# PEER mixer with 384 dense prompt columns instead of 416, gates from bf16 one-hots in three parts, and another layout of the scratch in HBM

## The chip, the cores and the metric

The kernel runs on one core of a Trainium2 chip, in one launch. The metric is the device time of that launch in microseconds (us), as the median of three runs. Engines are named as in the profile: PE (TensorE), DVE (VectorE), ACT (ScalarE), POOL (GpSimd), SP (SyncE, which here only issues DMAs).

## The reference

One inference step of a two-layer decoder: 512 prompt tokens and 8 sample tokens. Layer 0 mixes tokens with a chunked gMLP, layer 1 with sparse attention; behind each stands the PEER channel mixer, which is what the change is about. It finds 16 experts of 16384 for each of 8 heads of a token and adds up their outputs. The block is computed as:

```
PEER_HEADS = 8
N_KEYS = 128
PEER_TOPK = 16

        v1, i1 = lax.top_k(s1, PEER_TOPK)
        v2, i2 = lax.top_k(s2, PEER_TOPK)
        cand = (v1[..., :, None] + v2[..., None, :]).reshape(PEER_BLOCK, PEER_HEADS, PEER_TOPK * PEER_TOPK)
        cand_idx = (i1[..., :, None] * N_KEYS + i2[..., None, :]).reshape(PEER_BLOCK, PEER_HEADS, PEER_TOPK * PEER_TOPK)
        top_s, top_pos = lax.top_k(cand, PEER_TOPK)
        eidx = jnp.take_along_axis(cand_idx, top_pos, axis=-1)
        gate = jax.nn.softmax(top_s, axis=-1)
        u = expert_u[eidx]
        act = jax.nn.gelu(jnp.einsum('thkd,td->thk', u, xb))
        vv = expert_v[eidx]
        return jnp.einsum('thk,thkd->td', (gate * act).astype(vv.dtype), vv)
```

All numbers are float32. `expert_u` and `expert_v` have 16384 rows of 1024 numbers for each layer, 67 MB each.

## The kernel before

**Two ways to one sum.** For the last ND = 416 prompt tokens (the dense columns, `D0` to `TP`) the kernel computes the activations of all 16384 experts and multiplies them by a gate that is zero for those not chosen. For the first D0 = 96 prompt tokens and the 8 sample tokens (the sparse ones) it fetches the chosen rows alone. Activations are held transposed: experts on the partitions, tokens in the columns.

**Slabs.** The weights come in slabs of 128 x 1024 floats (512 KB). SP loads them into a ring of four `raw` buffers (L473; the next load of a buffer waits until the slab before it in that buffer is used). ACT rounds each to `w_hi` (L1104), POOL or, in the output stage, DVE makes the rest, `w_lo` (L2274, L1955), two slabs ahead of PE. A slab in `dense` (L638) is 24 matmuls: 8 pieces x (hi x hi, hi weights x low input, low weights x hi input), each with ND columns.

**The score stage of a layer (s0, s1: 128 slabs of `u`).** PE multiplies slab n (`s_slab`), ACT takes the gelu (L1236) and SP stores it to `act_d` (L513). Between the slabs the gates are made, by four blocks of 128 prompt tokens. A block has
- score matmuls of all keys (L814, 16 matmuls), which ACT copies to `sc` (L1288);
- a routing window of `ROUTE_SLABS` slabs (20, 16, 16, 16). In it DVE finds the 16 experts a head: `chosen` with its MAX8, FIND_INDEX8 and MATCH_REPLACE8 (L1711 to L1724), the sums of candidates `cand` (L1739), the sixteen rounds of L1773 and L1777, and `shares` (L1785 to L1789), which ends with `route_done`;
- three transposes of `route` (L825) on PE, which wait for `route_done`, and copies of them by ACT to `idxT` and `gateT` (L1309, L1313), which end with `slotT_done`;
- gate steps (`STEPS_OF`: 4 in block 0, since only its last 32 tokens are dense, then 16, 16, 16). In a step of 8 tokens PE does one slab and then 8 gate matmuls (`gates`, L774): for each token, a one-hot of the first key index by a one-hot of the second that carries the gate. Both one-hots are made by DVE (`one_hots`: L1873 for `hot`, L1876 eight times for `hot_gate`), in two buffers. They compare with `count_row`, a copy of `iota` in PSUM (the tile `misc`, L1799). ACT copies the result to `gout` (L1249), and SP stores each second step to `gate_d` (L524).

After the last gate step, the slabs left are plain (8 of them).

**The sparse tokens.** They are worked in groups of 16 entries of the list (`NGR` = 7 groups: one of the samples, six of 16 prompt tokens each), 16 picks a group, so NDOT = 112 dots and 112 values a layer. For each, POOL issues an indirect DMA that gathers 128 rows (64 for the samples) of 4 KB into one of four `rows` buffers (L2308). A dot is one DVE operation over 1024 elements (L1838), against the group's inputs, which lie in PSUM. They are laid out on SBUF by `group_rows` (`hS`, L1824) and turned by PE (`group_h`, L796). Which dot stands where is written in tables: 12 in each window (`WINDOW_DOTS`; DVE does one at each call of `between`, and there are 12 calls in a routing), `STEP_DOTS` in the gate steps. `FETCH_AT` puts each fetch on POOL two slabs before. The indices of the prompt's sparse tokens go by HBM: after block 0's `route_done` SP stores `route` to `route_d` (L530), waits for it, and reads it back in another order with 24 transfers (L534) into `routeP`, of which DVE makes `expertP` (L1913).

**The output stage (y0, y1: 128 slabs of `v`).** In groups of 8 slabs, ACT's queue loads the activations and gates back (`abuf`, `gbuf`), DVE multiplies them (`weigh`, L1940), ACT and POOL split the product (L1278, L2316), PE multiplies (L638), DVE adds to `x` (L1984). DVE also makes `w_lo` there and adds one gathered row a slab to the sum of the sparse group (`value`, L1857). A finished group goes by ACT to `v_out`, by PE (`group_y`, L843) to PSUM, by DVE to `x`. Eight weighings and eight low parts (L1947) stand before the first slab.

## Time and profile before

| | |
|---|---|
| time, median of 3 runs (lowest to highest) | 3715.84 us (3708.44 to 3722.89) |
| the profiled execution, its span | 3715.8 us |
| PE busy | 3517.8 us, 95% |
| DVE busy | 2481.2 us, 67% |
| ACT busy | 1361.9 us, 37% |
| POOL busy | 1842.5 us, 50% |
| s0, y0 | 439.9 to 1173.1 us, 1175.3 to 1774.2 us |
| s1, y1 | 2366.7 to 3095.2 us, 3097.4 to 3699.1 us |
| moved by DMA | 812.36 MB, mean 219 GB/s |

The stages are cut at the first and the last slab matmul (L638) of each. Busy time adds the instructions of an engine; a PE record of a pipelined matmul is longer than the step from one matmul to the next, so the rate is read from the starts. "Idle before" in brackets is the time an engine waited and what ended it.

### The profile page before, as it was taken

How to read it: one execution, taken by the hardware profiler on the slowest of the kernel's cores; microseconds unless marked ns; L12 is line 12 of the kernel's file. 1: busy time of each engine (PE TensorE's matmuls, PEld its weight loads, DVE VectorE, ACT ScalarE, POOL GpSimd, SP SyncE). 2: the span in 40 equal slices, each digit the busy share in tenths (PEclk: the TensorE clock that was granted, in tenths of full speed). 3: DMA queues.
4: the chain of work that ended last, by engine and by line, in shares of the span. 5: the costliest groups of instructions: out<-in, count | busy, mean ns of one | idle time of the engine just before them, and what ended most of it. 6: DMA issues, size and time to landing. Idle time of an engine off the chain costs nothing.

```text
span 3715.8 us, 61775 instructions
## 1 busy us (share of the span) xinstructions
PE 3517.8 (95%) x21277; PEld 3348.0 (90%) x21277; DVE 2481.2 (67%) x5400; ACT 1361.9 (37%) x1938; POOL 1842.5 (50%) x1172
## 2 busy tenths in 40 slices
PE   7999999999999999999888689999999999999998
PEld 7999999999999999999773359999999999999998
DVE  3342597777775777775678543679697876777774
ACT  3322343534444333333221353344435353333332
POOL 3434456555655555552541234456565655555551
PEclk9999999999999999999998699999999999999999
DMA  3222367877788999994346322467777879999982
GB/s 131 80 69 91 103 188 247 277 247 262 262 281 274 298 310 313 324 320 154 99 116 179 105 74 91 136 193 249 268 240 277 274 282 277 297 326 311 329 295 97
DMA packets 392484, 812.36 MB, mean 219 GB/s; under 512 B 52104, under 2 KB 249672, under 8 KB 384888
## 3 DMA queue, kind: packets, MB, share of 16 engines
q1 hardware_dynamic: 171600, 458.35, 37.0%
q0 software_dynamic: 64608, 230.73, 18.1%
q10 hardware_dynamic: 156048, 120.37, 11.0%
q8 instruction: 127, 2.08, 0.2%
q14 instruction: 101, 0.83, 0.1%
HBM read 695.39 MB, written 112.74 MB: 217 GB/s over the span
## 4 chain that ended last, share of the span: by engine, by line
PE 66%; DVE 16%; DMA 7%; issue 4%; ACT 2%; POOL 2%; SPq 2%; another core or an unknown queue 0%; ACTq 0%; DVEq 0%; POOLq 0%
PE acc L638 42%; PE acc L625 15%; DMA rows<-u_in,expertP 4%; PE misc L774 3%; DVE rows L1838 3%; DMA raw<-slabs_in 2%; POOL w_lo L2274 1%; DVE misc L1773 1%; DVE route L1777 1%; DVE hot_gate L1876 1%; PE misc L814 1%; ACT w_hi L1104 1%; DVE work L1716 1%; DVE keyi L1724 1%; PE misc L843 1%
## 5 line engine op out<-in xcount | busy, mean ns | idle before, releaser
L2274 POOL TENSOR_TENSOR w_lo<-raw,w_hi 128x1024 fp32r<-128x1024 f32 x365 | 892.6, 2446 | 1079.8 <-ACT w_hi L1104 1078.6
L638 PE MATMUL acc<-h_hi,w_hi 128*128 128x416 f32 x3072 | 1097.7, 357 | 0.2 <-POOL h_lo L2316 0.2
L638 PE MATMUL acc<-h_lo,w_hi 128*128 128x416 f32 x3072 | 1085.9, 353 | 0.0
L638 PE MATMUL acc<-h_hi,w_lo 128*128 128x416 f32 x3072 | 1081.2, 352 | 0.0
L1104 ACT ACTIVATE w_hi<-raw 128x1024 fp32r<-128x1024 f32 x617 | 653.3, 1060 | 1090.0 <-DMA raw<-slabs_in 1045.4
L638 PEld LDWEIGHTS acc<-h_hi,w_hi 128*128 128x128 f32 x3072 | 581.2, 189 | 8.5 <-POOL h_lo L2316 0.6
L638 PEld LDWEIGHTS acc<-h_hi,w_lo 128*128 128x128 f32 x3072 | 581.9, 189 | 7.4
L638 PEld LDWEIGHTS acc<-h_lo,w_hi 128*128 128x128 f32 x3072 | 581.3, 189 | 3.9
L1955 DVE TENSOR_TENSOR w_lo<-raw,w_hi 128x1024 fp32r<-128x1024 f32 x252 | 325.4, 1291 | 206.1 <-ACT w_hi L1104 205.5
L1838 DVE CUSTOM_DVE_ANT_0 rows<-acc,rows 128x1024 f32<-128x1024 f32 (+1 forms) x224 | 273.4, 1221 | 205.9 <-DMA rows<-u_in,expertP 183.7
L638 PE MATMUL acc<-y_hi,w_hi 128*128 128x416 f32 x1024 | 362.1, 354 | 10.3 <-DVE y_lo L1947 4.3
L1236 ACT ACTIVATE gelu<-acc 128x416 f32<-128x416 f32 x256 | 132.5, 517 | 649.1 <-PE acc L638 588.4
L638 PE MATMUL acc<-y_hi,w_lo 128*128 128x416 f32 x1024 | 361.3, 353 | 0.0
L638 PE MATMUL acc<-y_lo,w_hi 128*128 128x416 f32 x1024 | 358.4, 350 | 0.0
L2316 POOL TENSOR_TENSOR h_lo<-abuf,h_hi 128x416 fp32r<-128x416 f32 x128 | 208.6, 1630 | 234.2 <-ACT h_hi L1278 232.3
L2316 POOL TENSOR_TENSOR y_lo<-abuf,y_hi 128x416 fp32r<-128x416 f32 x112 | 180.2, 1609 | 234.0 <-ACT y_hi L1278 233.1
L1876 DVE TENSOR_SCALAR hot_gate<-misc,idxT,gateT 128x128 f32<-128x128 f32 x832 | 273.8, 400 | 0.0
L1984 DVE TENSOR_TENSOR x<-x,acc 128x416 f32<-128x416 f32 x256 | 148.9, 582 | 128.0 <-PE acc L638 122.3
L625 PE MATMUL acc<-h_hi,w_hi 128*128 128x260 f32 x912 | 191.7, 292 | 40.0 <-DVE rb L2019 16.7
L1249 ACT ACTIVATE gout<-misc 128x512 f32<-128x512 f32 x208 | 205.4, 1065 | 58.2 <-PE misc L774 50.9
L774 PEld LDWEIGHTS misc<-hot_gate,hot 128*128 128x128 f32 x1664 | 199.5, 191 | 30.1 <-issue 26.6
L774 PE MATMUL misc<-hot_gate,hot 128*128 128x128 f32 x1664 | 205.1, 276 | 20.9 <-DVE hot_gate L1876 14.0
(349 smaller groups left out, 5549.4 us busy)
## 6 DMA issues: line engine op xcount, KB each, us to landing
raw<-slabs_in SPq DMA_DIRECT2D x617, 512.0 KB
act_d<-gelu SPq DMA_DIRECT2D x256, 208.0 KB
gate_d<-gout SPq DMA_DIRECT2D x52, 1024.0 KB
abuf<-act_d ACTq DMA_DIRECT2D x32, 1664.0 KB
gbuf<-gate_d ACTq DMA_DIRECT2D x30, 1664.0 KB
unit<-ck_in SPq DMA_DIRECT2D x72, 128.0 KB
vquad<-cv_in SPq DMA_DIRECT2D x64, 128.0 KB
unit<-ck_in ACTq DMA_DIRECT2D x56, 128.0 KB
```

The costliest lines, as they stand in the source:

```text
L625: last = pe.matmul(acc[:, par, half, 0:HT], w[:, c, :], m(c)[:, half * HT:(half + 1) * HT], start=start and c == 0 and w is w_hi[r] and m ...
L638: last = pe.matmul(acc[:, 0, par, 0:ND], w[:, c, :], m(c), start=c == 0 and w is w_hi[r] and m is m_hi, stop=c == KC - 1 and w is w_lo[r])
L774: last = pe.matmul(misc[:, q, j * P:(j + 1) * P], hot1[par][:, t, :], hot_gate[par][:, t, :], start=True, stop=True)
L1104: act.activation(w_hi[r][:], raw[r][:], ACT.Copy).then_inc(hi_done, 1)
L1236: act.activation(gelu[:, par, :], acc[:, 0, par, 0:ND], ACT.Gelu_apprx_tanh).then_inc(acc_free_act, 1)
L1249: act.activation(gout[cpar][:, :, t0:t0 + 4].rearrange("p i t -> p t i"), misc[:, q, :].rearrange("p (t i) -> p t i", t=4), ACT.Copy).then ...
L1838: dve.tensor_tensor_reduce(out=row, in0=acc[0:n, 1], in1=row, scale=1.0, scalar=0.0, op0=ALU.mult, op1=ALU.add, accum_out=dots[0:n, g, k:k ...
L1876: last = dve.tensor_scalar(hot_gate[par][:, t, :], count_row, idxT[:, 1, t0 + t:t0 + t + 1], gateT[:, t0 + t:t0 + t + 1], ALU.is_equal, AL ...
L1955: dve.tensor_tensor(w_lo[r][:], raw[r][:], w_hi[r][:].bitcast(F32), ALU.subtract).then_inc(lo_done, 1)
L1984: dve.tensor_tensor(x[:, c, D0:TP], x[:, c, D0:TP], acc[:, 0, c % 2, 0:ND], ALU.add).then_inc(acc_free_dve, 1)
L2274: pool.tensor_tensor(w_lo[r][:], raw[r][:], w_hi[r][:].bitcast(F32), ALU.subtract).then_inc(lo_done, 1)
L2316: pool.tensor_tensor(y_lo[par][:, c, 0:ND], abuf[par][:, c, :], y_hi[par][:, c, 0:ND].bitcast(F32), ALU.subtract).then_inc(y_lo_done, 1)
```

## The change

- **Columns.** `ND` goes from 416 to 384, so `D0` from 96 to 128: block 0 is sparse as a whole. The sparse groups become 9 (`NGR`), dots and values 144 a layer each. Block 0 loses its transposes, copies and 4 gate steps; PE waits for its `route_done` ahead of block 1's score matmuls, since the same PSUM banks hold what DVE works on. Gate steps are 16 in each of blocks 1 to 3, and 12 plain slabs follow.
- **Tables.** 16 dots in block 0's window and 12 in the others, then 24 in each block's gate steps, and 20 behind the last. Values: 11 for each 9 slabs (`values_by`). The groups' ends follow from it (`GROUP_END`).
- **Order at the end of s.** DVE weighs the first group of eight before it makes `weights`, and ACT's gelu of the dots stands behind the last slab.
- **One-hots.** `idxT`, `gateT` and the one-hots become bf16, laid out with the 8 tokens of a step innermost; `iota8` is a bf16 count in SBUF in that form, made by one DVE copy at the start of `peer`. The gate is split into three bf16 parts (`gate_parts`, once a block). A step is five DVE operations of 128 x 1024 (two comparisons, three products), and on PE 24 matmuls of 128 columns, three for each token. `count_row` is gone.
- **Scratch.** `act_d` holds four slabs side by side for a partition and `gate_d` is ordered by the group that reads it, so that loads run over 6 KB and 12 KB in a row, while a store of gates has runs of 512 bytes.

```diff
@@ -49,7 +49,7 @@
-ND = 416
+ND = 384
@@ -218,33 +218,34 @@
-        topd = take("topd", [P, PH, TOPK])
...
+        topd = route[:, 2]
...
-        idxT = take("idxT", [P, 2, ND])
-        gateT = take("gateT", [P, ND])
+        idxT = take("idxT", [P, 2, ND], BF16)
+        gateT = take("gateT", [P, 3, ND], BF16)
+        iota8 = take("iota8", [P, P, TG // 2], BF16)
...
-        hot1 = [take(f"hot1_{r}", [P, HG, P]) for r in range(2)]
-        hot_gate = [take(f"hot_gate{r}", [P, HG, P]) for r in range(2)]
+        hot1 = [take(f"hot1_{r}", [P, P, HG], BF16) for r in range(2)]
+        hot_gate = [take(f"hot_gate{r}", [P, 3, P, HG], BF16) for r in range(2)]
@@ -365,8 +366,8 @@
-        act_d = [nc.dram_tensor(f"act_d{l}", [NK, P, ND], F32).ap() for l in range(2)]
-        gate_d = [nc.dram_tensor(f"gate_d{l}", [NG, P, NK, TG], F32).ap() for l in range(2)]
+        act_d = [nc.dram_tensor(f"act_d{l}", [NK // 4, P, 4, ND], F32).ap() for l in range(2)]
+        gate_d = [nc.dram_tensor(f"gate_d{l}", [NK // GRP, P, NG, GRP, TG], F32).ap() for l in range(2)]
@@ -452,17 +453,27 @@
-        WINDOW_DOTS = 12
-        STEP_DOTS = [[1] * 4, [1] * 4 + [0, 0] + [2, 1, 2, 1, 2, 2, 1, 2, 1, 2]]
...
+        WINDOW_DOTS = [16, 12, 12, 12]
+        STEP_DOTS = [[], [1] * 4 + [2] * 8 + [1] * 4, [1] * 8 + [2] * 8, [1, 2] * 8]
...
+        TAIL_DOTS = NDOT - len(at_slab)
+        at_slab += [S_DONE + i * (NK - S_DONE - 3) // TAIL_DOTS for i in range(TAIL_DOTS)]
...
+        def values_by(n):
...
+            return min(NDOT, ((n + 1) * 11 + 8) // 9)
...
+        at_slab += [NK + n for n in range(NK) for _ in range(values_by(n) - (values_by(n - 1) if n else 0))]
...
+        GROUP_END = [next(n for n in range(NK) if values_by(n) >= (g + 1) * TOPK) for g in range(NGR)]
@@ -521,7 +532,8 @@
-                    sp.dma_start(gate_d[l][chunk], gout[cpar][:]).then_inc(gate_stored[cpar], 16)
+                    sp.dma_start(gate_d[l][:, :, chunk].rearrange("j p g t -> p j (g t)"),
+                                 gout[cpar][:].rearrange("p (j g) t -> p j (g t)", g=GRP)).then_inc(gate_stored[cpar], 16)
@@ -771,8 +784,9 @@
-                            last = pe.matmul(misc[:, q, j * P:(j + 1) * P], hot1[par][:, t, :],
-                                             hot_gate[par][:, t, :], start=True, stop=True)
+                            for part in range(3):
+                                last = pe.matmul(misc[:, q, j * P:(j + 1) * P], hot1[par][:, :, t],
+                                                 hot_gate[par][:, part, :, t], start=part == 0, stop=part == 2)
@@ -796,18 +810,21 @@
+                    if b == 1:
+                        pe.wait_ge(route_done, B)
@@ -816,21 +833,43 @@
-                    s_only(2)
-                    group_h(2 * b - 1 if b else 0)
-                    s_only(ROUTE_SLABS[b] - 2)
+                        s_only(2)
+                        group_h(0)
+                        s_only(ROUTE_SLABS[0] - 2)
+                        continue
+                    if b == 1:
+                        s_only(2)
+                        group_h(1)
+                        s_only(ROUTE_SLABS[b] - 2)
+                    if b == 2:
+                        s_only(ROUTE_SLABS[b])
+                    if b == 3:
+                        s_only(12)
+                        group_h(6)
+                        s_only(ROUTE_SLABS[b] - 12)
...
-                    if b:
+                    if b == 1:
...
-                        group_h(2 * b)
-                        steps(b, 4, STEPS_OF[b] - 4)
-                    else:
-                        steps(b, 0, STEPS_OF[b])
+                        group_h(2)
+                        steps(b, 4, 12)
+                        group_h(3)
+                        steps(b, 12, 16)
+                    if b == 2:
+                        group_h(4)
+                        steps(b, 0, 12)
+                        group_h(5)
+                        steps(b, 12, 16)
+                    if b == 3:
+                        steps(b, 0, 8)
+                        group_h(7)
+                        steps(b, 8, 16)
+                s_only(2)
+                group_h(8)
@@ -1255,12 +1295,12 @@
-                    act.dma_start(abuf[par][:], act_d[l][j * GRP:(j + 1) * GRP].rearrange("i p t -> p i t")).then_inc(
+                    act.dma_start(abuf[par][:].rearrange("p (b i) t -> p b (i t)", b=2),
+                                  act_d[l][2 * j:2 * j + 2].rearrange("b p i t -> p b (i t)")).then_inc(
...
-                    act.dma_start(gbuf[par][:], gate_d[l][:, :, j * GRP:(j + 1) * GRP, :].rearrange(
-                        "n p i t -> p n i t")).then_inc(group_loaded[par], 16)
+                    act.dma_start(gbuf[par][:], gate_d[l][j]).then_inc(group_loaded[par], 16)
@@ -1295,22 +1334,25 @@
+                    if b == 0:
+                        continue
...
-                    act.activation(gateT[:, lo - D0:t0 + P - D0], misc[:, 2, 2 * P + lo - t0:3 * P], ACT.Copy).then_inc(
+                    act.activation(gateT[:, 0, lo - D0:t0 + P - D0], misc[:, 2, 2 * P + lo - t0:3 * P], ACT.Copy).then_inc(
@@ -1324,10 +1366,6 @@
-                act.wait_ge(rows_used, l * OPS + NDOT)
-                act.activation(dots[0:SR, 0], dots[0:SR, 0], ACT.Gelu_apprx_tanh).then_inc(dot_act_done, 1)
-                act.activation(dots[:, 1:NGR], dots[:, 1:NGR], ACT.Gelu_apprx_tanh).then_inc(dot_act_done, 1)
@@ -1349,6 +1387,10 @@
+                act.wait_ge(rows_used, l * OPS + NDOT)
+                act.activation(dots[0:SR, 0], dots[0:SR, 0], ACT.Gelu_apprx_tanh).then_inc(dot_act_done, 1)
+                act.activation(dots[:, 1:NGR], dots[:, 1:NGR], ACT.Gelu_apprx_tanh).then_inc(dot_act_done, 1)
@@ -1865,17 +1906,38 @@
+            def gate_parts(b):
...
+                t0 = max(b * P, D0)
+                c0, c1 = t0 - D0, (b + 1) * P - D0
+                gate = misc[:, 2, 2 * P + t0 - b * P:3 * P]
+                left = rest[:, t0 - b * P:P]
+                dve.tensor_tensor(left, gate, gateT[:, 0, c0:c1], ALU.subtract).then_inc(dve_step, step.up())
+                dve.wait_ge(dve_step, step.at)
+                dve.tensor_copy(gateT[:, 1, c0:c1], left).then_inc(dve_step, step.up())
+                dve.wait_ge(dve_step, step.at)
+                dve.tensor_tensor(gateT[:, 2, c0:c1], left, gateT[:, 1, c0:c1], ALU.subtract).then_inc(parts_done, 1)
+                dve.wait_ge(parts_done, n_parts[0] + 1)
+                n_parts[0] += 1
...
-                dve.tensor_tensor(hot1[par][:], count_row.unsqueeze(1).to_broadcast([P, HG, P]),
-                                  idxT[:, 0, t0:t0 + HG].unsqueeze(2).to_broadcast([P, HG, P]), ALU.is_equal)
-                for t in range(HG):
-                    last = dve.tensor_scalar(hot_gate[par][:, t, :], count_row, idxT[:, 1, t0 + t:t0 + t + 1],
-                                             gateT[:, t0 + t:t0 + t + 1], ALU.is_equal, ALU.mult)
-                last.then_inc(hot_done, 1)
+                of = [P, P, HG]
+                dve.tensor_tensor(hot_gate[par][:, 2], iota8[:], idxT[:, 1, t0:t0 + HG].unsqueeze(1).to_broadcast(of),
+                                  ALU.is_equal).then_inc(dve_step, step.up())
+                dve.tensor_tensor(hot1[par][:], iota8[:], idxT[:, 0, t0:t0 + HG].unsqueeze(1).to_broadcast(of),
+                                  ALU.is_equal)
+                dve.wait_ge(dve_step, step.at)
+                for part in range(2):
+                    dve.tensor_tensor(hot_gate[par][:, part], hot_gate[par][:, 2],
+                                      gateT[:, part, t0:t0 + HG].unsqueeze(1).to_broadcast(of),
+                                      ALU.mult).then_inc(dve_step, step.up())
+                dve.wait_ge(dve_step, step.at)
+                dve.tensor_tensor(hot_gate[par][:, 2], hot_gate[par][:, 2],
+                                  gateT[:, 2, t0:t0 + HG].unsqueeze(1).to_broadcast(of), ALU.mult).then_inc(hot_done, 1)
@@ -1918,13 +1983,17 @@
-                    dve.wait_ge(slotT_done, B + 1)
+                        continue
+                    dve.wait_ge(slotT_done, l * (NDB - 1) + b)
+                    gate_parts(b)
...
-                        for _ in range(STEP_DOTS[b > 0][r]):
+                        for _ in range(STEP_DOTS[b][r]):
...
+                while done[0] < NDOT:
+                    next_dot()
@@ -1955,15 +2024,15 @@
+                for c in range(GRP):
+                    weigh(0, c)
+                for c in range(GRP):
+                    low_part(0, c)
...
-                for c in range(GRP):
-                    weigh(0, c)
-                for c in range(GRP):
-                    low_part(0, c)
@@ -1974,10 +2043,10 @@
-                    if n < NDOT:
-                        value(l, n)
-                    if n % TOPK == 10 and 0 < n // TOPK <= NGR:
-                        group_add(l, n // TOPK - 1)
+                    for i in range(values_by(n - 1) if n else 0, values_by(n)):
+                        value(l, i)
+                    if n - 5 in GROUP_END:
+                        group_add(l, GROUP_END.index(n - 5))
```

On DVE, in a gate step of block 1 (`rows`, `dots`: a dot; `hot`, `hot_gate`: the one-hots; `iota_119` is `iota8`), before:

```order
L1838 ISA rows_133,dots<-acc,rows_133 64x1024
L1838 ISA dots 64x1
L1873 TENSOR_TENSOR hot_1_125<-misc,idxT 128x1024
L1876 TENSOR_SCALAR hot_gate_127<-misc,idxT,gateT 128x128 x8
L1913 SCALAR_TENSOR_TENSOR expertP<-routeP 128x96
```

and after:

```order
L1879 ISA rows_130,dots<-acc,rows_130 128x1024
L1879 ISA dots 128x1
L1929 TENSOR_TENSOR hot_gate_125<-iota_119,idxT 128x1024
L1931 TENSOR_TENSOR hot_0_123<-iota_119,idxT 128x1024
L1935 TENSOR_TENSOR hot_gate_125<-hot_gate_125,gateT 128x1024 x2
L1939 TENSOR_TENSOR hot_gate_125<-hot_gate_125,gateT 128x1024
```

One operation of 1024 elements that reads PSUM and eight of 128 have become five of 1024 elements with both inputs in SBUF. (The rows of before are the last step of block 0, which has the same form, with `expertP` behind it.)

On DVE, from the end of block 0's routing to the start of block 1's. Before, its last share (`route<-route,gsum`) is followed by the samples' shares and the first gate step; three more steps stand ahead of `expertP` and of the next MAX8:

```order
L1789 TENSOR_TENSOR route<-route,gsum 128x128
L1785 TENSOR_REDUCE gsumS<-routeS 64x1
L1787 RECIPROCAL gsumS<-gsumS 64x1
L1789 TENSOR_TENSOR routeS<-routeS,gsumS 64x16
L1838 ISA rows_130,dots<-acc,rows_130 64x1024
L1838 ISA dots 64x1
L1873 TENSOR_TENSOR hot_0_124<-misc,idxT 128x1024
L1876 TENSOR_SCALAR hot_gate_126<-misc,idxT,gateT 128x128 x8
```

After:

```order
L1831 TENSOR_TENSOR route<-route,gsum 128x128
L1879 ISA rows_129,dots<-acc,rows_129 64x1024
L1879 ISA dots 64x1
...
L1879 ISA rows_132,dots<-acc,rows_132 64x1024
L1879 ISA dots 64x1
L1827 TENSOR_REDUCE gsumS<-routeS 64x1
L1829 RECIPROCAL gsumS<-gsumS 64x1
L1831 TENSOR_TENSOR routeS<-routeS,gsumS 64x16
L1978 SCALAR_TENSOR_TENSOR expertP<-routeP 128x128
L1753 MAX keyv<-sc 128x8 x16
```

Four dots have moved behind the last share, and `expertP` follows them with no gate step between.

On DVE, at the end of the score stage. Before:

```order
L1873 TENSOR_TENSOR hot_1_125<-misc,idxT 128x1024
L1876 TENSOR_SCALAR hot_gate_127<-misc,idxT,gateT 128x128 x8
L1959 TENSOR_TENSOR weights<-dots,routeS 64x16
L1961 TENSOR_TENSOR weights<-dots,routeP 128x96
L1940 TENSOR_TENSOR abuf_146<-abuf_146,gbuf_147 128x416 x8
```

After, where twenty dots stand between the last one-hots and these rows:

```order
L1879 ISA rows_132,dots<-acc,rows_132 128x1024
L1879 ISA dots 128x1
L2009 TENSOR_TENSOR abuf_145<-abuf_145,gbuf_146 128x384 x8
L2016 TENSOR_TENSOR y_lo_148<-abuf_145,y_hi_147 128x384 x8
L2032 TENSOR_TENSOR weights<-dots,routeS 64x16
L2034 TENSOR_TENSOR weights<-dots,routeP 128x128
```

The weighing of the first eight slabs now stands behind all dots and ahead of `weights`.

## Rows read from the trace of the kernel before

**Rows 1.** The page: busy us and share of the span, by engine.

```profile
PE 3517.8 (95%) x21277; PEld 3348.0 (90%) x21277; DVE 2481.2 (67%) x5400; ACT 1361.9 (37%) x1938; POOL 1842.5 (50%) x1172
```

**Rows 2.** Stages by windows: length, busy PE, PEld, DVE, ACT, POOL, clock, DMA share, GB/s.

```profile
439.90:1173.10 733.20, 705.14 (x4071) 692.24 (x4069) 563.47 (x1730) 329.53 (x414) 417.52 (x241) 0.99 0.75 250
1175.30:1774.20 598.90, 596.89 (x3184) 588.68 (x3184) 431.67 (x496) 198.70 (x262) 314.77 (x232) 1.00 0.86 283
2366.70:3095.20 728.50, 702.55 (x4071) 689.78 (x4069) 563.36 (x1730) 328.97 (x415) 418.75 (x241) 0.99 0.75 251
```

**Rows 3.** Windows of s0: routing and gate steps of block 1, routing of block 2.

```profile
568.00:644.00 76.00, 73.40 (x392) 72.21 (x390) 63.42 (x265) 28.58 (x37) 53.35 (x30) 1.00 0.76 239
644.00:758.00 114.00, 109.10 (x685) 106.81 (x686) 84.30 (x185) 56.29 (x70) 55.36 (x34) 0.99 0.77 269
758.00:837.00 79.00, 73.61 (x392) 72.42 (x392) 65.89 (x265) 28.66 (x37) 52.90 (x30) 0.99 0.76 243
```

**Rows 4.** Timeline, end of block 2's window on PE; waits of DVE, 644 to 758.

```profile
836.76 0.90 PE L825 MATMUL misc<-ident,route 128*128 128x128 f32 x3 [5.39 <-DVE route L1789]
...
DVE rows L1838 <- DMA rows<-u_in,expertP: 20.8, 11, 5.8
```

**Rows 5.** Timeline of PE (start, length): matmuls of 260 and of 416 columns.

```profile
319.73 0.40 PE L625 MATMUL acc<-g_hi,w_hi 128*128 128x260 f32 x2
319.97 0.40 PE L625 MATMUL acc<-g_lo,w_hi 128*128 128x260 f32 x2
...
1499.95 0.35 PE L638 MATMUL acc<-y_hi,w_lo 128*128 128x416 f32 x1
1500.14 0.35 PE L638 MATMUL acc<-y_hi,w_hi 128*128 128x416 f32 x1
```

**Rows 6.** Timeline, hand-over from block 0 to block 1, on DVE, SP and POOL.

```profile
529.61 1.89 DVE L1789 TENSOR_TENSOR route<-route,gsum 128x128 f32<-128x128 f32 x1
...
533.24 0.33 SPq L530 DMA_DIRECT2D route_d<-route  x1
538.56 12.94 SPq L534 DMA_DIRECT2D routeP<-route_d  x24
...
553.25 0.24 DVE L1913 SCALAR_TENSOR_TENSOR expertP<-routeP 128x96 uint32<-128x96 f32 x1
568.50 0.29 DVE L1799 COPY misc<-iota 128x128 f32<-128x128 f32 x1 [15.01 <-ACT sc L1288]
...
576.57 0.97 POOL L2308 DMA_INDIRECT rows<-u_in,expertP  x1
...
582.34 1.22 DVE L1838 CUSTOM_DVE_ANT_0 rows<-acc,rows 128x1024 f32<-128x1024 f32 x1 [10.46 <-DMA rows<-u_in,expertP]
```

**Rows 7.** Timeline of one gate step of block 2, on PE, DVE, ACT and POOL.

```profile
884.29 2.05 PE L774 MATMUL misc<-hot_gate,hot 128*128 128x128 f32 x16 [1.01 <-DVE hot_gate L1876]
886.09 0.43 PE L638 MATMUL acc<-h_hi,w_hi 128*128 128x416 f32 x1
...
886.36 1.21 DVE L1873 TENSOR_TENSOR hot<-misc,idxT 128x1024 f32<-128x1024 f32 x1
887.49 2.63 DVE L1876 TENSOR_SCALAR hot_gate<-misc,idxT,gateT 128x128 f32<-128x128 f32 x8
890.04 1.21 DVE L1838 CUSTOM_DVE_ANT_0 rows<-acc,rows 128x1024 f32<-128x1024 f32 x1
...
893.54 1.08 ACT L1104 ACTIVATE w_hi<-raw 128x1024 fp32r<-128x1024 f32 x1
...
894.70 2.41 POOL L2274 TENSOR_TENSOR w_lo<-raw,w_hi 128x1024 fp32r<-128x1024 f32 x1 [2.81 <-ACT w_hi L1104]
```

**Rows 8.** Timeline: a cast, `cand` without and behind POOL's `w_lo`, a tensor_tensor.

```profile
512.24 0.42 DVE L1777 TENSOR_TENSOR route<-misc,route 128x256 f32<-128x256 f32 x1
...
604.63 1.15 DVE L1739 TENSOR_TENSOR cand<-keyv 128x512 f32<-128x512 f32 x2
...
796.34 0.29 DVE L1733 CAST keyf<-keyi 128x256 f32<-128x256 uint32 x1
796.55 3.36 DVE L1739 TENSOR_TENSOR cand<-keyv 128x512 f32<-128x512 f32 x2
...
796.88 2.61 POOL L2274 TENSOR_TENSOR w_lo<-raw,w_hi 128x1024 fp32r<-128x1024 f32 x1 [1.27 <-ACT w_hi L1104]
```

**Rows 9.** The page: queues (packets, MB, share); then y0's first window.

```profile
q1 hardware_dynamic: 171600, 458.35, 37.0%
q0 software_dynamic: 64608, 230.73, 18.1%
q10 hardware_dynamic: 156048, 120.37, 11.0%
...
1173.00:1300.00 127.00, 123.11 (x644) 120.31 (x644) 91.98 (x107) 41.20 (x56) 74.36 (x55) 0.99 0.96 290
```

58 lines of the change are left out of this document (32 added, 26 removed).

## The prediction

> **What bounds the kernel now.** I read the engine line of the page first: PE is busy for 95% of the span [rows 1]. A busy PE alone does not say what a narrower matmul is worth, so I cut the span by stage [rows 2]: in each layer the score stage (s, 128 slabs through `s_slab`) takes 733 or 729 us and the output stage (y, 128 slabs) 599 or 602, together 2662 of 3715.8 us. In y PE is all but continuously busy. In s it is not, and the stretches tell why [rows 3]. A block of 128 prompt tokens has two parts: a routing window of 16 slabs, in which DVE picks experts, and 16 gate steps, each a slab and eight gate matmuls. Block 2's window ends with PE waiting 5.4 us for DVE's last routing row [rows 4]. So windows are DVE's, gate steps and y are PE's.
>
> **Columns: 416 to 384.** Matmuls of 416 columns start 0.19 us apart, those of 260 columns 0.12 [rows 5]. The line through both gives 0.45 ns a column, so 32 columns are 14 ns, and a slab of 24 matmuls takes 4.22 us in place of 24 x 0.19 = 4.56. For 512 slabs that is 174 us if PE set the pace everywhere. What is left of it is the question.
>
> **Windows of blocks 2 and 3** (78 us each, [rows 3]) are not shortened: PE's 16 slabs get 5.5 us faster and it waits 5.5 us longer. DVE's own work is the same 12 dots and the same picks. Its first dot waits 10.5 us (block 1's in [rows 6]) for rows that Pool asks for one slab into the window; that slab is 0.3 us shorter. I take -0.5 us a window, -1 a layer.
>
> **The hand-over from block 0.** Before, four gate steps and block 1's scores stand between DVE's `route_done` (531.5) and its next routing (568.5) [rows 6]. Now block 0 has no gate steps. What is late next is `routeP`: SP stores the routes at 533.24, waits until 538.56 and issues 24 transfers for 12.94 us, to 551.50; with some 2 us of landing (an estimate, from the `expertP` row at 553.25, which may have found them already there) DVE can go on at 553.5, 22 us after `route_done`. Four more dots (4 x 1.22) lie behind `route_done` and inside this wait, so they cost nothing. The copy into `iota8` costs about 1.2 us ahead of it (as the 1024-element rows of [rows 7]). SP issues no slab loads meanwhile, but PE has 15 us of slack here. Block 1's first dot then waits about 2 us and not 10.5, as Pool can fetch right behind `expertP` (0.97 to issue at 576.57, 4.8 to land by 582.34, less 3.2 of MAX8). Sum: DVE starts 15 - 1.2 = 14 us earlier and needs 8 us less: **-22 us**.
>
> **Gate steps.** From 644 to 758 us are block 1's 16 steps and block 2's scores, 114 us [rows 3]. Three changes:
> - PE: the slab, -0.34. The gate matmuls were 16 records in 1.8 us, from 884.29 to the next slab's matmul at 886.09 [rows 7]; now 24 matmuls of 128 columns in one pass. The line of rows 5 gives 62 ns for 128 columns, 1.5 us; the fp32 record's 0.112 us gives 2.7. All operands are now read with a step of 16 bytes, which no row shows. I stay between, at 1.8, and count no change: it leans to the line, as the operands are no longer fp32.
> - DVE: one `hot` of 1.13 and eight `hot_gate`, 3.68 us from 886.36 to 890.04, become five tensor_tensor of 1024 bf16 elements. At the fp32 rate they are 1.14 apart, at two elements a cycle 0.60. That the engine has such a rate is seen in the cast of 256 elements in 0.29 us, while a tensor_tensor of 256 takes 0.42 [rows 8]. I take 0.60: 3.2 us with two waits. Dots rise from 1.25 to 1.5 a step, 1.8 us. Total 5.1 us against PE's 4.22 + 1.8 = 6.0, so nothing on the path.
> - Three small operations of `gate_parts` (about 0.9 us with their waits) stand before the first one-hots of a block. Before, the first one-hots were there 1.4 (waiting) + 1.2 (a dot) + 3.7 = 6.3 us after the route, now 1.4 + 0.9 + 1.2 + 3.2 = 6.7; and PE, which already waited for them, is there 0.34 earlier. So PE waits 0.8 more a block. One more `group_h` is 0.9.
>
> A block's steps: -5.5 + 0.8 + 0.9 = **-3.8 us**, three blocks **-11**.
>
> The Trainium skill ("VectorE: DVE Perf Modes", The perf-mode tier table) gives a bf16 tensor_tensor from SBUF twice the fp32 rate; no operation of the kernel before shows it, and by the page the sum would stay as above.
>
> **The tail of s.** Slabs left after the last gate step are 12, not 8: 12 x 4.22 - 8 x 4.56 = +14.2, and one `group_h`, 0.9. This is where the four steps saved in block 0 come back as plain slabs. Twenty dots lie there now, two for each slab. Behind them stand the eight weightings that the y stage needs; I add 4 us of late start. Tail: **+19**. Two dots a step also load the DMA queues more; +5 for rows that come late (in block 1's steps DVE already waits 20.8 us for rows [rows 4], but it has slack).
>
> s stage: -22 - 1 - 11 + 19 + 5 = **-10 us** a layer. Most of the narrower matmul is given back, to DVE in the windows.
>
> **The y stage.** PE: -128 x 0.34 = -44; two more `group_y` with 1.8 us of PE each, +3.5. DMA: of [rows 9], q10 moves 120.4 MB for 11.0% of 16 engines, 18.4 GB/s an engine; q1 20.8, q0 21.4. One y stage before: 67 MB of slabs, 55 MB of activations and gates (at q10's rate) and 55 MB of expert rows, 8730 engine-us, 546 us of the 599. After: 50 MB in long runs at q1's rate, 71 MB of expert rows: 8980, 561 us, while PE's time falls to 599 - 44 + 3.5 = 559. The measured share (0.86 of 599 is 515) is 0.94 of what this reckoning gives, so 529 of 559. It is full, not over. I add 5 us for slabs that come late. DVE, a slab: 0.50 + 1.14 + 0.47 + 1.22 values x 1.21 = 3.6 (starts 0.07 us before the one ahead ends, lengths as n/0.96 + 0.07 us fits the rows of [rows 7]), under 4.22. y: -44 + 3.5 + 5 = **-35 us** a layer.
>
> **Sum**: 2 x (-10 - 35) = -90, so 3715.8 - 90 = 3626 us. The profiled execution (3715.8) is the median of the runs (3715.84). Under 0.5% (19 us) a measurement of this kernel can't tell a change from none.
>
> **Rivals.**
> 1. *Gate matmuls at 0.112 us.* Reading every eighth bf16 may hold PE at the fp32 pace or below. 24 x 0.112 = 2.7, +0.9 on 96 steps = +86: **3712**, no change. Against it: an fp32 element takes two passes, bf16 one. The Trainium skill ("Advanced Engine Details and Errata", Memory Cachelines) says that SBUF lines have 16 bytes and an access that hits a new line each time pays; here each element of both operands is on a line of its own. No row shows its price. Chance 0.17.
> 2. *Transfers set y's pace.* The share is 0.96 in y's first 127 us now [rows 9]. If it can't rise, y stays near 599 us: 3626 + 70 = **3696**, at the edge of no change. Chance 0.11.
> 3. *The port between DVE and Pool (slower).* `cand` reads two SBUF operands, and the second of its two operations came behind Pool's `w_lo`: 3.36 us for two, where they take 1.2 when Pool is idle [rows 8]. So one waits for the other to end. The one-hots before read `misc` (PSUM); all five now read SBUF twice, and Pool's 2.4 us `w_lo` comes in each step, at 894.70, 1.1 us after `w_hi` [rows 7]. Alone this fits: 3.2 + 2.4 = 5.6 of 6.0, with the dots (PSUM and SBUF) under `w_lo`. It decides when dots come late by more than the 2.6 us by which DVE is ahead: then `w_lo` falls into the burst in each step and a step is 3.2 + 2.4 + 1.9 = 7.5, +1.5 on 96 steps = +144: **3770**. Chance 0.10.
> 4. *The fast rate isn't taken* (the change does not do what it says, also slower). Five at 1.14 and Pool's 2.4 shut out of them: 8.3 a step, +2.3 x 96 = +221: **3847**. For it: one operand of each is a row of eight read again and again, of which the trace has none. Chance 0.06.
>
> **How the numbers follow.** Forecast 3626, its own range 3585 to 3672 (gate matmuls at 62 ns give 3599, late rows and a late start of y up to +45), chance 0.56. Range for 8 in 10: from 3585 to 3765, which takes in rivals 1 and 2 and the milder half of 3. Faster by over 0.5% (below 3697): the forecast, and part of rivals 1 and 2, 0.65. Within: 0.18. Slower: rivals 3 and 4 and the top of 1, 0.17.
>
> **What would show it.** Matmuls of 384 columns 175 ns apart. PE waiting at `route_done` for 6 to 8 us in block 0, 12 to 16 in block 1, some 10 in blocks 2 and 3. The DVE tensor_tensor of the one-hots at 0.6 to 0.7 us; many over 2 us would be rival 3, all at 1.2 rival 4. The gap between a gate step's slabs, 1.8 us now: over 2.5 is rival 1. In y, slab starts 4.22 us apart; if the DMA share is at 0.97 and PE idles before slabs, rival 2. Wrong would be above all the assumption that DVE's windows don't move, and that the dots' rows keep up.

## The result: 4273.6 us, 15% slower

The changed kernel takes 4273.58 us (median of 4 runs, 4269.2 to 4275.98) against 3716.28: a ratio of 1.150, 95% interval 1.148 to 1.153. The forecast was 3626, its range ended at 3765. The profiled execution has a span of 4270.4 us, and its stages are cut as before.

The engine line of the page, of after (it answers to [rows 1]):

```profile
PE 3921.3 (92%) x22007; PEld 3557.3 (83%) x22007; DVE 2701.8 (63%) x5156; ACT 1354.8 (32%) x1922; POOL 1929.7 (45%) x1300
```

PE is busy for 404 us more, though its slab matmuls are narrower. The windows view by stage, of after (columns as in [rows 2]; y0, y1, s0, s1):

```profile
1424.00:2054.00 630.00, 579.53 (x3216) 568.45 (x3216) 488.23 (x532) 198.34 (x264) 308.76 (x263) 0.97 0.81 289
3628.60:4257.60 629.00, 579.98 (x3216) 571.78 (x3216) 477.71 (x529) 192.14 (x255) 311.20 (x261) 0.97 0.81 287
440.80:1420.70 979.90, 925.57 (x4404) 815.04 (x4402) 620.04 (x1571) 326.07 (x402) 461.94 (x274) 0.86 0.62 200
2643.10:3625.40 982.30, 924.22 (x4403) 813.21 (x4402) 624.01 (x1570) 325.93 (x402) 463.06 (x274) 0.85 0.62 199
```

Each s stage is 247 to 254 us longer (733 and 729 before), each y stage 31 and 27 longer (599 and 602). These add up to 559 us, and the spans differ by 555: nothing outside the stages grew. In s the granted clock is down from 0.99 to 0.86, in y the DMA share from 0.86 to 0.81. Inside s0, routing of block 1, gate steps of block 1 with block 2's scores, and routing of block 2, the windows that answer to [rows 3]:

```profile
557.00:627.00 70.00, 55.78 (x303) 54.84 (x301) 62.97 (x265) 24.53 (x32) 48.07 (x28) 0.93 0.82 270
627.00:824.00 197.00, 191.00 (x826) 155.72 (x827) 99.84 (x135) 59.24 (x71) 63.38 (x38) 0.78 0.51 160
824.00:896.00 72.00, 66.61 (x380) 66.29 (x380) 60.06 (x263) 27.73 (x36) 51.76 (x30) 0.98 0.81 263
```

The two routing windows are 6 and 7 us shorter. The gate steps take 197 us where they took 114. One of them on PE, by the timeline (it answers to [rows 7]):

```profile
716.83 0.34 PE L651 MATMUL acc<-h_lo,w_hi 128*128 128x384 f32 x1
717.00 0.34 PE L651 MATMUL acc<-h_hi,w_lo 128*128 128x384 f32 x1
717.18 5.81 PE L788 MATMUL misc<-hot_gate,hot 128*128 128x128 bf16 x24
722.63 0.68 PE L651 MATMUL acc<-h_hi,w_hi 128*128 128x384 f32 x1
723.11 0.52 PE L651 MATMUL acc<-h_lo,w_hi 128*128 128x384 f32 x1
723.43 0.52 PE L651 MATMUL acc<-h_hi,w_lo 128*128 128x384 f32 x1
```

From the first gate matmul (717.18) to the next slab (722.63) it is 5.45 us, 0.227 us a matmul; before, the eight took 1.8 in [rows 7] and 1.70 in the median. Then the clock counts as well: slab matmuls start 0.32 us apart behind the gate matmuls (723.11, 723.43), and 0.17 to 0.18 apart at the slab's end (716.83, 717.00), when the upper level is granted again. In 84 of the 96 steps it is 5.43 to 5.46 us: in 4 of them the granted clock stayed at its upper level (2.4 GHz), in 80 it was at the lower (1.2 GHz) for a part. In the other 12 something else of PE's stands before the next slab. Behind the gate matmuls the lower level held for 3.3 us in the median step. The median step is 11.29 us long against 6.31.

### The profile page after: what moved, and what is told of

Same layout as the page of the kernel before. It is cut to its first block, busy times and chain, and to the rows that moved or that the text cites. A ratio compares the mean times of both kernels' runs of the same rounds, so it can differ in the third digit from the quotient of the medians.

```text
span 4270.4 us, 63212 instructions
## 1 busy us (share of the span) xinstructions
PE 3921.3 (92%) x22007; PEld 3557.3 (83%) x22007; DVE 2701.8 (63%) x5156; ACT 1354.8 (32%) x1922; POOL 1929.7 (45%) x1300
## 4 chain that ended last, share of the span: by engine, by line
PE 56%; DVE 22%; DMA 11%; issue 5%; ACT 2%; POOL 2%; SPq 1%; another core or an unknown queue 0%; DVEq 0%; ACTq 0%; POOLq 0%
PE acc L651 24%; PE acc L638 13%; PE misc L788 13%; DMA raw<-slabs_in 8%; DVE rows L1879 3%; DVE w_lo L2024 2%; DMA rows<-u_in,expertP 2%; DVE route L1819 1%; DVE misc L1815 1%; DVE abuf L2009 1%; ACT w_hi L1144 1%; DVE work L1758 1%; DVE keyi L1766 1%; DVE keyi L1757 1%; DVE keyv L1762 1%
## 5 line engine op out<-in xcount | busy, mean ns | idle before, releaser
L651 PE MATMUL acc<-h_hi,w_hi 128*128 128x384 f32 x3072 | 1143.1, 372 | 95.1 <-POOL w_lo L2344 41.8
L651 PE MATMUL acc<-h_lo,w_hi 128*128 128x384 f32 x3072 | 1108.1, 361 | 0.0
L651 PE MATMUL acc<-h_hi,w_lo 128*128 128x384 f32 x3072 | 1105.9, 360 | 0.0
L788 PE MATMUL misc<-hot_gate,hot 128*128 128x128 bf16 x2304 | 557.3, 414 | 18.3 <-DVE hot_gate L1939 18.3
L788 PEld LDWEIGHTS misc<-hot_gate,hot 128*128 128x128 bf16 x2304 | 327.5, 146 | 218.5 <-issue 35.7
L651 PE MATMUL acc<-y_hi,w_hi 128*128 128x384 f32 x1024 | 357.9, 350 | 57.9 <-DVE x L2053 43.3
L2378 POOL DMA_INDIRECT rows<-v_in,expertP x256 | 260.3, 1017 | 232.4 <-DVE misc L1898 103.5
L651 PE MATMUL acc<-y_lo,w_hi 128*128 128x384 f32 x1024 | 354.0, 346 | 0.0
L651 PE MATMUL acc<-y_hi,w_lo 128*128 128x384 f32 x1024 | 353.6, 345 | 0.0
L2378 POOL DMA_INDIRECT rows<-u_in,expertP x256 | 267.9, 1047 | 84.8 <-issue 28.3
```

Source lines behind the costliest of these rows:

```text
L651: last = pe.matmul(acc[:, 0, par, 0:ND], w[:, c, :], m(c), start=c == 0 and w is w_hi[r] and m is m_hi, stop=c == KC - 1 and w is w_lo[r])
L788: last = pe.matmul(misc[:, q, j * P:(j + 1) * P], hot1[par][:, :, t], hot_gate[par][:, part, :, t], start=part == 0, stop=part == 2)
L2378: pool.indirect_dma_start(out=rows[n % RB][0:rows_of], out_offset=None, in_=a[f"v{l}" if half else f"u{l}"], in_offset=bass.IndirectOffset ...
```

## Experiments

All are variants of the changed kernel. "A step" is a gate step, "gates" the time from its first gate matmul to the next slab, in the median. Lengths of stages are those of the profiled execution. Where the text gives no ratio, the time is that of one execution.

| kernel | time, us | gates, us | s0, s1 | y0, y1 |
|---|---|---|---|---|
| before | 3716 | 1.70 | 733, 729 | 599, 602 |
| changed | 4274 | 5.45 | 980, 982 | 630, 629 |
| both operands in a row | 3869 | 1.32 | 780, 775 | 631, 627 |
| moving operand in a row | 3872 | 1.51 | 772, 779 | 636, 631 |
| weights in a row | 4244 | 5.25 | 961, 969 | 634, 626 |
| moving operand, step of 8 bytes | 3918 | 2.87 | 800, 802 | 631, 632 |
| moving operand, step of 4 bytes | 3872 | 1.55 | 784, 775 | 633, 627 |
| roles exchanged | 3912 | 1.51 | 796, 803 | 631, 632 |
| exchanged, other DVE order | 3801 | 1.51 | 749, 747 | 622, 630 |
| scratch of before | 4165 | 5.45 | 970, 979 | 584, 579 |
| long loads in pieces | 4181 | 5.45 | 978, 982 | 587, 584 |
| exchanged, order, scratch of before | 3702 | 1.51 | 736, 741 | 589, 587 |
| exchanged, order, pieces | 3719 | 1.51 | 748, 748 | 585, 584 |
| exchanged, order, hybrid scratch | 3701 | 1.51 | 745, 741 | 586, 584 |
| columns alone | 3702 | 1.80 | 734, 741 | 597, 586 |
| exchanged, order, scratch of before, half the rows | 3703 | 1.51 | 731, 736 | 618, 611 |
| the same, all rows, half the values | 3639 | 1.51 | 739, 732 | 573, 581 |
| exchanged, order, pieces, half the values | 3687 | 1.51 | 742, 741 | 574, 574 |

### What makes the gate matmuls slow

PE reads 128 elements in a row, which belong to other tokens, so these kernels compute other gates; nothing else is changed. The first does it for both operands, the next two for one each:

```diff
-  hot1[par][:, :, t],  hot_gate[par][:, part, :, t]
+  hot1[par][:].rearrange("p k t -> p (k t)")[:, t * P:(t + 1) * P],
+  hot_gate[par][:, part].rearrange("p k t -> p (k t)")[:, t * P:(t + 1) * P]
```

> The changed kernel, but PE reads both operands of the gate matmuls as 128 elements in a row instead of every eighth. The elements are then those of other tokens, so the gates are wrong; DVE, the number of matmuls and all else stay. Theory 1 (the step of 16 bytes between elements is what costs): the 24 gate matmuls of a step fall from 5.45 us to 1.5 to 1.8 us, the clock stays at its upper level in the gate steps, a step falls from 11.3 to about 6 us, and the time from 4274 to about 3755 us (96 x 5.3 less). Theory 2 (24 bf16 matmuls with 24 weight loads cost this in any layout): 5.45 us stays and the time stays at 4274.

> As the run before, but only the moving operand (hot_gate) is read in a row; the weights (hot) keep the step of 16 bytes. Part of the gates is wrong. If the moving operand pays, the 24 matmuls fall to 1.5 to 1.8 us and the time to about 3755; if the weights pay, both stay (5.45 us, 4274). If each alone is slow and the load of weights runs beside the matmul before it, neither run with one operand in a row gains.

> The other half: only the weights (hot) are read in a row, the moving operand keeps the step of 16 bytes. Part of the gates is wrong. If the moving operand pays alone, 5.45 us and 4274 stay; if the weights pay alone, 1.5 to 1.8 us and about 3755.

The moving operand in a row alone takes the gates from 5.45 to 1.51 us and the time from 4274 to 3872; the weights alone take them to 5.25 and the time to 4244. So 24 matmuls and 24 loads of weights are not slow as such, and strided weights cost 0.2 us a step. It is the moving operand, of which a column was fetched every 16 bytes. With it in a row the clock is 0.95 over the run (0.91 in the changed kernel); it fell behind the gate matmuls of 14 steps of 96, and of 92 in the changed kernel: the fall of the clock went with the slow matmuls. The time stopped at 3870, though, 115 us above the 3755 that I had expected. The y stages are as they were, and the expectation had left them so; the 115 us are gate steps of 7.5 us where I had expected 6, which comes below. That other elements are read here is not what makes it fast: the kernels with exchanged roles below compute the right gates and take the same 1.51 us.

```diff
-  hot_gate[par][:, part, :, t]
+  hot_gate[par][:, part].rearrange("p k t -> p (k t)")[:, t * 64:t * 64 + 509:4]   # or 255:2
```

> The changed kernel, but PE reads the moving operand of the gate matmuls with a step of 8 bytes (every fourth bf16) in place of 16; the weights keep 16. The elements are then other ones, so the gates are wrong; all else stays. Theory 1 (each 16-byte piece of SBUF that is opened for one element costs; two elements in one are enough): the 24 matmuls take about 1.5 us and the time is 3872, as with the moving operand in a row. Theory 2 (any step between elements costs, in proportion to the bytes passed over): about 2.7 us, the time about 4000. Theory 3 (any step costs the whole): 5.45 us and 4274.

> The same with a step of 4 bytes (every second bf16). Theory 1: 1.5 us and 3872, as with 8 bytes. Theory 2: 1.5 us (1.36 by proportion, under the rate in a row), 3872. Theory 3: 5.45 us and 4274.

With steps of 16, 8, 4 and 2 bytes the gates take 5.45, 2.87, 1.55 and 1.51 us, so 1.77, 0.93, 0.50 and 0.49 ns a column. The cost goes with the bytes that are passed over, and from 4 bytes down the matmul's own pace rules. Two elements in each 16 bytes are not enough: theory 1 gave 1.5 us for the step of 8 bytes, theory 2 gave 2.7. The time of that kernel, 3918, is 82 us under theory 2's 4000: I had left out the clock, which fell behind the gate matmuls of only 19 of 96 steps here. The Trainium skill ("Advanced Engine Details and Errata", Memory Cachelines) says that one needs two hits on a line of 16 bytes; the trace agrees that one element in 16 bytes is bad (1.77 ns a column against 0.49) and disagrees on two (0.93).

### DVE and POOL shut each other out

With both operands in a row, steps with one dot took from 5.6 us up, those with two dots mostly 7.6. The timeline of such a step in that kernel, DVE, then POOL, then PE:

```profile
695.91 1.22 DVE L1879 CUSTOM_DVE_ANT_0 rows<-acc,rows 128x1024 f32<-128x1024 f32 x1
697.06 0.69 DVE L1929 TENSOR_TENSOR hot_gate<-iota,idxT 128x1024 bf16<-128x1024 bf16 x1
697.66 0.68 DVE L1931 TENSOR_TENSOR hot<-iota,idxT 128x1024 bf16<-128x1024 bf16 x1
698.26 3.47 DVE L1935 TENSOR_TENSOR hot_gate<-hot_gate,gateT 128x1024 bf16<-128x1024 bf16 x2
701.77 0.69 DVE L1939 TENSOR_TENSOR hot_gate<-hot_gate,gateT 128x1024 bf16<-128x1024 bf16 x1
...
698.79 2.40 POOL L2344 TENSOR_TENSOR w_lo<-raw,w_hi 128x1024 fp32r<-128x1024 f32 x1 [2.60 <-ACT w_hi L1144]
...
702.60 0.62 PE L788 MATMUL misc<-hot_gate,hot 128*128 128x128 bf16 x8 [1.84 <-DVE hot_gate L1939]
```

Two products take 3.47 us here and 1.28 to 1.33 elsewhere, with POOL's `w_lo` of 2.40 inside them, and PE waits 1.84 us for the last. It is no single case: in s0 of this kernel, 19 of the 96 first and second products ran beside `w_lo` for over 0.5 us and took 2.88 us in the median, the 57 that never met it 0.68. The dots, which read PSUM and SBUF, took 1.22 beside it (57 of them) and without it (76). The place repeats in each step, since the four engines wait for each other in a ring: `w_lo` for ACT's `w_hi`, ACT for the gate matmuls, PE for DVE, DVE for `w_lo`. That is rival 3 of the prediction, at 7.6 us a step where it said 7.5, but not under its condition, which was that dots come late. Two kernels test it. The first swaps the roles of the one-hots, so that the one in rows moves; the second also changes DVE's order and lets the one in rows read its count from PSUM:

```diff
 # roles exchanged
-  pe.matmul(misc[...], hot1[par][:, :, t], hot_gate[par][:, part, :, t], ...)
+  pe.matmul(misc[...], hot_gate[par][:, part, :, t], hot1[par][:, t, :], ...)
-  dve.tensor_tensor(hot1[par][:], iota8[:], idxT[:, 0, t0:t0 + HG].unsqueeze(1)...)
+  dve.tensor_tensor(hot1[par][:], iota[:].unsqueeze(1)..., idxT[:, 1, t0:t0 + HG].unsqueeze(2)...)
 # other order: comparison and three products, the dots, and last
+  dve.tensor_tensor(hot1[par][:], count_in_psum.unsqueeze(1)..., idxT[:, 1, t0:t0 + HG].unsqueeze(2)...)
```

> The changed kernel with the two one-hots of a token in exchanged roles: the one that carries the three gate parts is loaded as weights, still with a step of 16 bytes, and the other is made in rows (fp32 count in SBUF, bf16 out) and moves. Same numbers, same order, scratch as changed. Theory (only the moving operand's step costs): 24 matmuls in 1.5 us instead of 5.45. With one two-input operation at 1.14 us more in place of one at 0.6, the port theory (DVE's two-SBUF-input operations and POOL's w_lo shut each other out) gives steps with two dots at 3.6 + 2.4 + 1.9 = 7.9 us or more and those with one dot at 6.5 to 7, the time 3890 to 3930. If the port plays no part, DVE needs 5.3 us and PE 5.8 a step, the time is about 3800.

> As the run with exchanged roles, and DVE in another order: the four operations with two SBUF inputs first, then the step's dots, then the one-hot in rows, whose count is read from PSUM, as in the kernel before. So 3.5 us of DVE's work a step have a PSUM input and can lie beside POOL's w_lo of 2.4 us. The port theory gives steps of 5.8 to 6.0 us with one dot or two, and a time of about 3790 us; if the excess over 5.8 us in the steps had another cause (rows that come late, ACT's copies), they stay at 7.6 with two dots and the time at 3870 or more.

The first took 3912 us with a median step of 8.12, the second 3801 with 6.42; both are as the port theory had them, within 11 us. DVE of the second, with two dots in the step (POOL's `w_lo` below it):

```profile
881.17 0.69 DVE L1939 TENSOR_TENSOR hot_gate<-hot_gate,gateT 128x1024 bf16<-128x1024 bf16 x1
881.78 1.22 DVE L1879 CUSTOM_DVE_ANT_0 rows<-acc,rows 128x1024 f32<-128x1024 f32 x1
...
882.92 1.22 DVE L1879 CUSTOM_DVE_ANT_0 rows<-acc,rows 128x1024 f32<-128x1024 f32 x1
...
884.07 1.22 DVE L1943 TENSOR_TENSOR hot<-misc,idxT 128x1024 bf16<-128x1024 f32 x1
885.21 1.39 DVE L1931 TENSOR_TENSOR hot_gate<-iota,idxT 128x1024 bf16<-128x1024 bf16 x1
...
883.65 2.40 POOL L2347 TENSOR_TENSOR w_lo<-raw,w_hi 128x1024 fp32r<-128x1024 f32 x1 [2.31 <-ACT w_hi L1144]
```

POOL's 2.4 us now lie beside a dot and the `hot` that reads PSUM, and nearly nothing is lost: only the comparison at 885.21, which begins before `w_lo` ends (886.05), takes 1.39 in place of 0.68. So 111 us went, with the same number of operations on DVE in a step. Order and source of the operand were changed together, and no run parts them. Steps stay at 6.4 where I had said 6.0, as DVE is busy without a break in those with two dots (6.70 in the median, 5.81 with one).

### The long runs in the scratch

> The changed kernel with act_d and gate_d laid out and loaded as in the kernel before (runs of 1.5 KB and 512 bytes), all else as changed. Theory A (a group's 3 MB in long packets push the slabs' 4 KB packets back, so that slabs come late in bursts): each y stage falls from 630 to about 575 us, the time to about 4165. Theory B (the sum of bytes, with two more groups of gathered rows, sets y's pace): y stays at 630 or grows, the time is 4274 or more.

The time fell to 4165, as theory A had it, and y to 584 and 579, 4 to 9 us above it. The page's queues (packets, MB, share of the span), first of after, then of that kernel:

```profile
q1 hardware_dynamic: 264784, 450.16, 32.1%
q10 hardware_dynamic: 29328, 111.98, 7.1%
```

```profile
q1 hardware_dynamic: 172624, 450.16, 31.6%
q10 hardware_dynamic: 147856, 111.98, 9.2%
```

The long runs do what they are for: q10 moves the same 112 MB in 7.1% of the 16 engines' time and not in 9.2%. But while they move, the slabs get less. The timeline of the changed kernel in y0, behind the load of a group (ACT, DVE, PE):

```profile
1706.17 0.39 ACTq L1298 DMA_DIRECT2D abuf<-act_d  x1
1706.59 0.49 ACTq L1303 DMA_DIRECT2D gbuf<-gate_d  x1
...
1721.70 1.06 ACT L1144 ACTIVATE w_hi<-raw 128x1024 fp32r<-128x1024 f32 x1 [11.62 <-DMA raw<-slabs_in]
...
1722.79 1.22 DVE L2024 TENSOR_TENSOR w_lo<-raw,w_hi 128x1024 fp32r<-128x1024 f32 x1 [6.62 <-ACT w_hi L1144]
1723.94 2.67 DVE L1898 SCALAR_TENSOR_TENSOR misc<-rows,weights,misc 128x1024 f32<-128x1024 f32 x2
1726.52 0.55 DVE L2053 TENSOR_TENSOR x<-x,acc 128x384 f32<-128x384 f32 x1
...
1727.21 0.66 PE L651 MATMUL acc<-h_hi,w_hi 128*128 128x384 f32 x1 [3.93 <-DVE x L2053]
```

From 1708 to 1720 q10's packets (6 and 12 KB) move 0.42 to 0.49 MB in each 2 us. The slab that SP asks for at 1710.84 has its 128 packets (4 KB) between 1714.5 and 1719.9, at 0.16 to 0.20 MB in 2 us, where one of 0.52 MB is wanted every 4.2 us. ACT waits 11.62 us for it, DVE 6.62 for ACT's half, and PE 3.93 for DVE's `x`, which stands on DVE behind the late `w_lo` and two values. Over y0 PE has 9 waits of over 2 us, and 2 with the scratch of before.

That the load comes in one piece is not enough to explain it. The scratch of before is loaded in one piece too, 3.1 MB a group, but in packets of 1.5 KB and 512 bytes. From 2 to 14 us behind each request these move 0.32 MB in 2 us and leave the slabs 0.18; the long ones move 0.48 and leave 0.14 (means over the 13 groups of y0). Asking in pieces, with the layout in HBM as changed, makes the runs shorter too, 3 KB:

```diff
-  act.dma_start(abuf[par][:]..., act_d[l][2 * j:2 * j + 2]...); act.dma_start(gbuf[par][:], gate_d[l][j])
+  # with each of the first four slabs of a group, k = 0 to 3
+  act.dma_start(abuf[par][:, 2 * k:2 * k + 2, :], act_d[l][2 * j + k // 2][:, 2 * (k % 2):2 * (k % 2) + 2, :])
+  act.dma_start(gbuf[par][:, 6 * k:6 * k + 6], gate_d[l][j][:, 6 * k:6 * k + 6])
```

> The changed kernel with its scratch layout, but a group's 3 MB are asked for in eight pieces of 375 KB (3 KB runs), two with each of the first four slabs of a group, where all stood before the first slab. If slabs come late because one long load goes ahead of them, each y falls from 630 to 565 to 580 us and the time is 4145 to 4175. If the long runs harm the slabs wherever they stand, y stays at 630 and the time at 4274.

y is 587 and 584, so the long runs in HBM do no harm when the load is cut up. Whether the spread over four slabs does it or the shorter packets, this kernel does not tell: it changed both. The time, 4181, is 6 us over the range that I gave, and y 4 to 7 over its own.

### Putting the parts together

> The run in the other order, with act_d and gate_d laid out and loaded as in the kernel before. If the two costs are independent, each y falls from 630 to about 580 us and the time is about 3685, 0.9% under the kernel before. If POOL and the DMA queues, freed in s, only move the wait, it is 3720 or more.

> The run with exchanged roles and the other order on DVE, with the long runs of the changed scratch and the pieces spread over four slabs. Against the same kernel with the scratch of before (3702 us, y 588 and 587): the DMA engines have less to do for the same bytes, so if the transfers set y's pace there, y is 565 to 575 and the time 3665 to 3680; if the spread doesn't help, y is 625 and the time 3800; if something else holds y at 588, 3702.

With the scratch of before: 3702.45 us, ratio 0.997 (0.995 to 0.998). With the pieces: 3718.93, ratio 1.002 (1.000 to 1.004). The y stages are alike (589 and 587, 585 and 584), so the DMA time that the long runs save brought next to nothing there; s is 7 to 12 us longer with the changed scratch. Gates laid out as before and activations in the changed layout:

> All computed. The same kernel with whole values, activations in the changed layout (long runs, loaded in pieces over four slabs) and gates in the layout of before (a store of 1 MB in runs of 8 KB, loads in pieces of 512-byte runs). If the stores of gates in runs of 512 bytes are what made s 748 us with the changed scratch and 736 to 740 with that of before, s is 738 here; y should be 580 to 587. The time is then 3685 to 3700, 0.4 to 0.8% under the kernel before. If s stays at 748, it is about 3715.

3701.07, ratio 0.998 (0.997 to 1.000), s 745 and 741: about half of the excess is gone, where I had said all (738). That the stores of gates in 512-byte runs are behind it is likely, and not shown by this.

### The columns alone

The one-hots, gate matmuls and scratch are those of the kernel before; `ND`, the tables and the order at the end of s are changed.

> The columns and tables of the changed kernel alone: 384 dense columns, nine sparse groups, the new order at the end of s; the one-hots (fp32, in rows, DVE reads the count from PSUM), the gate matmuls and the scratch are those of the kernel before. From the changed kernel's trace the hand-over gives 12 us a layer, the windows 14, the tail costs 29. Theory 1 (DVE sets the gate steps: 4.8 us of one-hots and 1.5 dots of 1.22, 6.6 us against 6.31 before): s 747, y 582, in all 1329 a layer against 1332 before, the time about 3710. Theory 2 (PE sets them: 4.22 + 1.7 = 5.9 us): s 714, the time about 3645.

3701.81 us, ratio 0.997 (0.995 to 0.998): theory 1, though its parts are off (s 734 and 741, not 747; y 597 and 586, not 582). The profiled execution is the slowest of ten, 3714, so its stages hold some 12 us more than the median one. A median step is 6.15 us and the mean 6.74, against 6.31 and 6.62 before; the narrower slab is given back in the steps with two dots, 7.09 us in the median. The gain of the columns is 12 us in all (the kernel before took 3714 beside it), not the 90 that I had forecast for the whole.

### What holds y at 585

> The kernel with exchanged roles, the other order and the scratch of before, but each of the 128 gathers of prompt rows in y fetches 64 of its 128 rows (the other half of the sum is wrong): 34 MB less of some 170 a y stage, DVE's and PE's work unchanged. There y takes 587 to 589 us with 38 us of gaps between slabs, of which nine group_y of 1.7 us are 15. Theory 1 (late transfers make the rest of the gaps): y falls to 560 to 565. Theory 2 (DVE, with 1.2 values a slab, and the engines that hang on it make them): y stays at 587. The time: 3650 or 3702.

> The same kernel, all rows fetched, but from the third on each value of DVE covers 512 of its 1024 elements (the sum is wrong in the others): some 0.5 us less of DVE for each of 144 values a y stage. Theory 1 (late transfers): y stays at 587, the time at 3702. Theory 2 (DVE): y falls to 560 to 570, the time to about 3660.

> The kernel with exchanged roles, the other order and the long loads in pieces (y 585 and 584 us, DMA busy 0.93), and from the third on each value of DVE covers half its elements (the sum is wrong in the others). With the scratch of before the same halving took y from 588 to 573 and 581, with the DMA engines busy for 0.96 to 1.00. If y is held by both, DVE's turn where DMA has room, and DMA where it has none, y falls here to 560 to 568. If DMA alone holds it, or something not named yet, y stays at 580 or more.

The first two were run where the kernel before took 3670 us and not 3710, and their time outside the four stages is 999 and 1003 us where it is 1045 in the same kernel with whole rows and values. So their times are not to be compared with the others; the stages are (s 731 to 739 us, against 736 and 741 in that kernel).

Half of the gathered rows left out made y longer, 618 and 611 us, which neither theory had: the packets of these gathers, which now land on 64 partitions only, took 258 ns in the median of y0 and not 159, and the DMA engines stayed busy for 0.93 to 0.99 at 247 to 263 GB/s instead of 337. The gathers of the samples, of 64 rows in every kernel, agree: 219 to 246 ns in y0 of the kernel before, the changed one and the one that this is made from, and 159 in s0, where the DMA share is 0.61 to 0.64. Fewer bytes did not empty the DMA engines, then, and the run isn't a test of fewer transfers. Half values took y to 573 and 581 with the scratch of before and to 574 and 574 with the pieces. The windows view of these two, one window of y0 each (columns as in [rows 2]), first with the scratch of before:

```profile
1310.00:1440.00 130.00, 127.65 (x740) 126.45 (x739) 94.83 (x129) 45.75 (x62) 82.17 (x66) 1.00 1.00 347
```

```profile
1320.00:1450.00 130.00, 129.43 (x752) 128.82 (x751) 96.51 (x130) 45.64 (x62) 82.81 (x67) 1.00 0.94 347
```

So DVE's turn is worth 10 us of y where DMA has room (share 0.94). With a share of 1.00 it is worth 6 and 16 in the two stages. Down to 564 there are 10 us that no run explains.

## Why the prediction was wrong

**Gate matmuls: the step that failed.** I put 24 of them at 1.8 us, between 1.5 (the line through [rows 5]) and 2.7 (the pitch of a fp32 record). They took 5.45. The prediction said itself that all operands are read with a step of 16 bytes, "which no row shows", and then bounded the unknown with the prices of operands in a row. The upper end was no bound: nothing in the trace held it there. Rival 1 named the cause and priced it at the same 2.7. The runs show 1.51 with the moving operand in a row, under my 1.8, and 5.45 with its step of 16 bytes: the price is in how it is read, and not in the number of matmuls or loads.

**The clock was not in the sum.** A slab behind slow gate matmuls starts at 0.32 us a matmul. Of the 5.0 us that a median step lost, 3.75 are the gate matmuls (5.45 less 1.70), and the slab took 5.84 us (11.29 less 5.45) where 4.2 was expected, so 1.6 are the clock: the lower level held for 3.3 us behind the gate matmuls, in which a slab matmul takes 0.32 us and not 0.175, and that costs 1.5.

**DVE: size right, order missed.** The five operations run at the fast rate as taken (0.69 and 0.68 us, 0.60 apart), so rival 4 is out. The port (rival 3, chance 0.10) is real: where PE is fast enough to show it, steps with two dots take 7.6 us, where rival 3's sum said 7.5. In the changed kernel itself the products already take 2.86 us beside `w_lo`, and it hides under the slow matmuls. I had argued that `w_lo` would fall beside the dots; in the ring of waits it falls on the products. Order and the source of one operand were worth 111 us.

**Windows.** I took -0.5 us for each of blocks 2 and 3; from 78.2 and 77.4 us they went to 71.9 and 75.2. It is the port again, by chance on the good side: before, block 2's two `cand` took 3.4 us and its `hS` 3.2 beside `w_lo`; after, `cand` met none (1.3) and `hS` lies outside the window. In block 3 `hS` went from 3.5 to 1.2 us. The wait for the first dot stayed, as said: 10.46 us in [rows 6] for block 1 before, 10.10 in block 2 after.

```profile
837.08 1.23 DVE L1879 CUSTOM_DVE_ANT_0 rows<-acc,rows 128x1024 f32<-128x1024 f32 x1 [10.10 <-DMA rows<-u_in,expertP]
```

**Hand-over: right in kind, -15.5 and not -22.** From `route_done` to block 1's routing it is 27.2 us in place of 37.0, and block 1's window 69.8 in place of 75.4. The timeline of after, which answers to [rows 6]:

```profile
539.64 0.33 SPq L542 DMA_DIRECT2D route_d<-route  x1
543.33 12.41 SPq L546 DMA_DIRECT2D routeP<-route_d  x24
...
556.97 0.29 DVE L1978 SCALAR_TENSOR_TENSOR expertP<-routeP 128x128 uint32<-128x128 f32 x1 [21.76 <-DMA routeP<-route_d]
557.18 3.18 DVE L1753 MAX8 keyv<-sc 128x8 f32<-128x128 f32 x16
565.80 1.23 DVE L1879 CUSTOM_DVE_ANT_0 rows<-acc,rows 128x1024 f32<-128x1024 f32 x1 [5.44 <-DMA rows<-u_in,expertP]
```

`routeP` is what is late next, as said. But SP reached the store of the routes at 539.64, 6 us later than before though the routes were done 1.5 us earlier: it stands behind a store of activations (issued at 539.07) that waits for its slab. That was one of the queues that I should have walked through. And the first dot waited 5.44, not 2.

**The tail of s.** From the end of the last gate matmuls to y it is 72 us where it was 39, so +33 against my +19 and +5. The waits view of after, 1352 to 1424.5:

```profile
DVE rows L1879 <- DMA rows<-u_in,expertP: 32.0, 14, 6.4
ACT w_hi L1144 <- DMA raw<-slabs_in: 18.5, 7, 3.4
PE acc L651 <- POOL w_lo L2344: 10.1, 5, 4.1
```

DVE waits for gathered rows at 14 of the twenty dots, but little of that reaches PE: y starts 3.3 us late. What PE waits for is `w_lo`, 10.1 us, and that goes back to ACT's `w_hi` and to slabs that come late, a term that I had at nothing. The clock, 0.91 there, is the rest (some 6 us). The tail of before had 2.2 us of waits on PE.

**The sum of s.** Hand-over -15.5, windows -8.5 and tail +33 leave 238 of the 247 us by which s0 grew, and that is 48 gate steps at 5.0.

**The y stage: -35 forecast, +31 and +27 measured.** Two mis-sized parts. The long packets of the group loads are 45 us a stage (629 to 584), and were not in the sum, which counted the DMA engines' time and not the order in which slabs get it. Without them y is 584 and not 564: DVE's turn is 10 of that.

Together: from 4274 the moving operand's step is 401 us (to 3872), exchanged roles and DVE's order against the port together 71 (to 3801), the changed scratch 99 (to 3702). What is left is 12 us under before, and so is the kernel with the columns alone. The parts that were added to help DVE and DMA are worth nothing measurable here once they are repaired: each of them took off what was not the last to end.

## What to carry to other kernels

A layout that gives DVE its fast rate is paid by whoever reads it next. Before a matmul's moving operand gets a step, measure that matmul by itself, or exchange the roles so that the strided operand is the weights. Where the trace has no row for a resource, the nearest row is not a bound, and the range has to be open on that side. A large load in long packets takes more than its share from a steady stream beside it: ask for it in pieces with shorter runs, or leave its packets short.

## What the runs showed of the hardware

- A bf16 moving operand costs 1.77 ns a column with a step of 16 bytes, 0.93 with 8, 0.50 with 4 and 0.49 in a row (weights with a step of 16 bytes in all four), at the same cost whether the granted clock stayed at its upper level or fell on the way (5.43 to 5.46 us for 24 either way, step of 16 bytes). Weights with a step of 16 bytes cost 0.2 us in 24.
- The granted clock was at its lower level (1.2 of 2.4 GHz) behind 92 of 96 runs of slow matmuls, though PE's row shows it busy without a gap; behind 24 matmuls in 1.5 us it was so in 14 of 96.
- A DVE tensor_tensor with both inputs in SBUF took 2.88 us beside POOL's `w_lo` of 2.4 and 0.68 alone (both operands in a row, s0); with one input in PSUM DVE lost nothing (1.22 both ways).
- DVE's tensor_tensor of bf16 elements in SBUF, one operand a row of eight read again and again, ran at 0.60 us for 1024 elements; the one-hot in rows, with a fp32 count in PSUM and the index broadcast innermost, at 1.14.
- Gathered rows of 4 KB that landed on 64 partitions took 219 to 258 ns a packet in y0, and 159 on 128 partitions; with the DMA engines less busy, in s0, 159 on 64 partitions too.
- 3.1 MB in packets of 6 and 12 KB moved at 0.48 MB in 2 us and left the slabs' 4 KB packets 0.14; in packets of 0.5 and 1.5 KB at 0.32, and left them 0.18.
